# Second memory attention of an encoder kernel, in pairs of heads woven into the projection slots

## What is computed

```python
def memory_attention(q, mem_k, mem_v):
    s = jnp.einsum('bthd,bmhd->bhtm', q, mem_k).astype(jnp.float32) * (MEM_HEAD_DIM ** -0.5)
    p = jax.nn.softmax(s, axis=-1).astype(mem_v.dtype)
    o = jnp.einsum('bhtm,bmhd->bthd', p, mem_v)
    return o.reshape(q.shape[0], q.shape[1], MEM_WIDTH)
...
            u = rms_norm(h, odd_norm1[j])
            q, k, v, g, zf, zb, qm = jnp.split(u @ odd_w_in[j], splits, axis=-1)
...
            mo = memory_attention(qm.reshape(B, T, MEM_HEADS, MEM_HEAD_DIM), mem_k, mem_v)
            h = h + jnp.concatenate([mix, mo], axis=-1) @ odd_w_out[j]
            h = h + moe_swiglu(rms_norm(h, odd_norm2[j]), odd_w_router[j], odd_w_gate[j], odd_w_up[j], odd_w_down[j])
```

## Time and profile before

| | |
|---|---|
| three runs | 1540.44, 1543.67, 1546.06 us; median 1543.67 |
| the profiled execution | 1542.09 us, its span 1540.3 us |
| TensorE | 1482.5 us busy, 96% of the span |
| VectorE, ScalarE | 1176.5 us (76%), 977.2 us (63%) |
| DMA queue of the weights | 427.79 MB, 77.4% of 16 engines |
| from G2's end to the first GLA product | 426.31 to 465.25 us |

### The profile page before, as it was taken

The page is one execution under the profiler, slowest core; times in us unless marked ns, Lnnn a source line. Parts: engine busy times, 40 slices in busy tenths (PEclk is TensorE's granted clock), DMA queues, the critical chain, the costliest instruction groups (busy, mean ns, idle before and its releaser), DMA issues.

```text
span 1540.3 us, 20865 instructions
## 1 busy us (share of the span) xinstructions
PE 1482.5 (96%) x7832; PEld 1256.6 (82%) x7832; DVE 1176.5 (76%) x1004; ACT 977.2 (63%) x907; POOL 20.5 (1%) x41
## 2 busy tenths in 40 slices
PE   5999999999988899999999999999999999999997
PEld 5985899998976688888888888888888888888885
DVE  4457554445556588888888889888889898888887
ACT  3337434443652377777777777777777777777775
POOL 1000000000001000000000000000000000000000
PEclk9999999999999899999999999999999999999999
DMA  7650465644350589989989989989998998998982
GB/s 271 228 165 1 142 203 191 191 149 128 125 191 28 192 323 381 375 313 379 370 312 377 368 316 371 379 313 369 377 366 319 378 371 311 377 372 310 382 318 94
DMA packets 198731, 428.41 MB, mean 278 GB/s; under 512 B 9534, under 2 KB 39580, under 8 KB 198685
## 3 DMA queue, kind: packets, MB, share of 16 engines
q1 hardware_dynamic: 198684, 427.79, 77.4%
HBM read 426.71 MB, written 1.05 MB: 278 GB/s over the span
## 4 chain that ended last, share of the span: by engine, by line
PE 89%; DVE 4%; ACT 3%; issue 2%; SPq 0%; DMA 0%; POOL 0%; DVEq 0%; ACTq 0%; POOLq 0%
PE ps L1234 27%; PE ps L1236 27%; PE ps L1235 27%; PE ps L1616 1%; DVE w_lo L1182 1%; PE ps L1335 1%; PE ps L1585 1%; ACT w_hi L717 1%; PE ps L1660 1%; PE ps L1309 1%; PE ps L1346 1%; PE ps L1255 1%; PE ps L1323 1%; ACT w_hi L514 0%; PE ps L1553 0%
## 5 line engine op out<-in xcount | busy, mean ns | idle before, releaser
L1182 DVE TENSOR_TENSOR w_lo<-raw,w_hi 128x2048 fp32r<-128x2048 f32 (+1 forms) x224 | 442.6, 1985 | 61.5 <-ACT w_hi L717 61.0
L717 ACT ACTIVATE w_hi<-raw 128x2048 fp32r<-128x2048 f32 (+1 forms) x224 | 372.7, 1672 | 130.3 <-PE ps L1236 130.2
L1234 PE MATMUL ps<-w_hi,xt_hi 128*128 128x512 f32 (+2 forms) x1080 | 418.5, 387 | 3.7 <-DVE xt_lo L1069 1.5
L1236 PE MATMUL ps<-w_hi,xt_lo 128*128 128x512 f32 (+2 forms) x1080 | 411.8, 381 | 0.0
L1235 PE MATMUL ps<-w_lo,xt_hi 128*128 128x512 f32 (+2 forms) x1080 | 410.9, 380 | 0.0
L1182 DVE TENSOR_TENSOR w_lo<-arena,w_hi 128x2048 fp32r<-128x2048 f32 x144 | 295.7, 2053 | 29.5 <-ACT w_hi L717 29.0
L717 ACT ACTIVATE w_hi<-arena 128x2048 fp32r<-128x2048 f32 x144 | 248.6, 1726 | 82.4 <-PE ps L1236 82.2
L821 DVE TENSOR_TENSOR w_lo<-raw,w_hi 128x2048 fp32r<-128x2048 f32 (+2 forms) x69 | 149.7, 2172 | 165.3 <-ACT w_hi L514 165.2
L1234 PEld LDWEIGHTS ps<-w_hi,xt_hi 128*128 128x128 f32 x1080 | 203.6, 189 | 44.5 <-issue 3.8
L1236 PEld LDWEIGHTS ps<-w_hi,xt_lo 128*128 128x128 f32 x1080 | 203.4, 188 | 38.4
L1235 PEld LDWEIGHTS ps<-w_lo,xt_hi 128*128 128x128 f32 x1080 | 203.9, 189 | 35.2
(11 more groups left out here) (204 smaller groups left out, 1205.4 us busy)
## 6 DMA issues: line engine op xcount, KB each, us to landing
raw<-exp_gate SPq DMA_DIRECT2D x74, 1024.0 KB, 5.8
raw<-exp_up SPq DMA_DIRECT2D x48, 1024.0 KB, 5.7
arena<-exp_down SPq DMA_DIRECT2D x48, 1024.0 KB, 5.6
arena<-exp_up SPq DMA_DIRECT2D x40, 1024.0 KB, 7.2
raw<-exp_down SPq DMA_DIRECT2D x40, 1024.0 KB, 6.3
arena<-exp_gate SPq DMA_DIRECT2D x24, 1024.0 KB, 6.8
raw<-exp_up SPq DMA_DIRECT2D x32, 512.0 KB, 4.8
raw<-even_gate SPq DMA_DIRECT2D x11, 1024.0 KB, 5.3
```

The source lines that it names most:

```text
L717: ins = act.activation(w_hi[:, n % CUT, at:at + src.shape[1]], src, ACT.Copy)
L1182: ins = dve.tensor_tensor(w_lo[:, n % CUT, cols], src, w_hi[:, n % CUT, cols].bitcast(F32), ALU.subtract)
L1234: pe.matmul(dst, a[0], b[0], start=start, stop=False, skip_group_check=shared)
L1236: return pe.matmul(dst, a[1], b[0], start=False, stop=stop, skip_group_check=shared)
```

## The change

- The factor 1/8 moves into ScalarE's copy of the memory queries (`qm1`), so the scores need no scaling. VectorE takes the maximum and ScalarE the exponential straight from the bank of the scores; the two scaled copies of each head are gone.
- The heads go in pairs. Both heads' scores are multiplied together, the two row halves of the array in turn; the two heads' products with the values likewise, the two column halves in turn.
- The pairs start one block sooner: scores of the first pair between G2 and G3, its transposes and the scores of the second pair between V0 and V1, its product behind V1, the transposes of the second pair between V2 and V3, its product behind V3.
- Turned probabilities have two banks, 6 and 7. The second half of V2 and V3 goes to bank 0 in place of bank 7, so V2 now waits for the copies of V0 and V1 (`in1_copied_a` 6, `in1_copied_v` 3).
- V0 waits for the first Silu eviction (`in1_copied_a` 4), no longer for the second. ScalarE takes the exponentials of the first pair ahead of the second Silu, and those of the second pair behind it.
- The second pair's scores wait for the exponentials of the first, which read the same banks.

```diff
--- before.py
+++ after.py
@@ -619,7 +619,8 @@
                 return ps[0:DK, bank, :].rearrange("p (h t) -> p h t", h=2)
 
             products(I_Z + 1)
-            act.activation(qm1.rearrange("p i t -> p (i t)"), ps[:, 5, :], ACT.Copy).then_inc(in1_copied_a, 1)
+            act.activation(qm1.rearrange("p i t -> p (i t)"), ps[:, 5, :], ACT.Copy,
+                           scale=float(HEAD) ** -0.5).then_inc(in1_copied_a, 1)
             products(I_Q + 1)
             act.activation(qg[0:DK, 0:2, :], pair_of(qg, 0), ACT.Copy, scale=float(DK) ** -0.5).then_inc(in1_copied_a, 1)
             for i in range(4):
@@ -654,19 +655,46 @@
             for d in range(2):
                 act.wait_ge(kd_turned, 2 * d + 2)
                 act.activation(kdt[:, d], ps[:, 4 + 2 * d:6 + 2 * d, 0:KW], ACT.Copy).then_inc(kdt_ready, 1)
+            def mem1_exp(p):
+
+                for i in (16 + 2 * p, 17 + 2 * p):
+                    act.wait_ge(scores_max, i + 1)
+                    if i == 19:
+                        act.wait_ge(probs_turned, 17)
+                    for t in range(TT):
+                        act.activation(s_b[:, i % 3, t, :], ps[:, 4 + i % 2, T * t:T * (t + 1)], ACT.Exp,
+                                       bias=stat[:, i, t, 0:1],
+                                       accum_out=stat[:, i, t, 1:2]).then_inc(probs_exp, 1)
+
+            def mem1_probs(p):
+
+                for i in (16 + 2 * p, 17 + 2 * p):
+                    act.wait_ge(probs_turned, i + 1)
+                    if p == 1:
+                        act.wait_ge(heads_done, i - 1)
+                    act.activation(pT_b[:, i % 2].rearrange("p j q -> p (j q)"), ps[:, 6 + i % 2, :],
+                                   ACT.Copy).then_inc(probsT_ready, 1)
+
+            def mem1_high(p):
+
+                act.wait_ge(heads_done, 18 + 2 * p)
+                act.activation(hT_hi[:, 0, T * p:T * (p + 1)], ps[:, 3, 0:T], ACT.Copy).then_inc(mix_hi, 1)
+
+            high_to(I_V + 1)
+            mem1_exp(0)
             gates_silu(1)
-            attention(16, 4, s_b, pT_b, range(0, 1))
-            high_to(I_V + CUT)
-            attention(16, 4, s_b, pT_b, range(1, 2))
+            high_to(I_V + 3)
+            mem1_probs(0)
+            mem1_exp(1)
             act.wait_ge(slot_done, I_V + 2)
             act.activation(v1[:, 0, 0:384], ps[:, 0, 0:384], ACT.Copy).then_inc(in1_copied_a, 1)
-            high_to(I_V + 1 + CUT)
-            attention(16, 4, s_b, pT_b, range(2, 3))
-            high_to(I_V + 2 + CUT)
-            attention(16, 4, s_b, pT_b, range(3, 4))
+            high_to(I_V + 4)
+            mem1_high(0)
+            high_to(I_V + 5)
+            mem1_probs(1)
             act.wait_ge(slot_done, I_V + 4)
             act.activation(v1[:, 0, 384:768], ps[:, 2, 0:384], ACT.Copy).then_inc(in1_copied_a, 1)
-            attention(16, 4, s_b, pT_b, range(4, 7))
+            mem1_high(1)
             high_to(I_V + 3 + CUT)
 
             def heads_high(b):
@@ -996,24 +1024,50 @@
                     dve.wait_ge(exps_done, 2 * d + x + 1)
                     dve.tensor_tensor(dst[0:DK, d], dst[0:DK, d], src[0:DK].rearrange("p h t -> p (h t)"),
                                       ALU.mult).then_inc(qk_ready, 1)
-            low_to(I_G + 3 + CUT)
-            attention(16, 4, s_b, 8, range(0, 1))
-            low_to(I_V + CUT)
+            def mem1_max(p):
+
+                for i in (16 + 2 * p, 17 + 2 * p):
+                    dve.wait_ge(scores_done, i + 1)
+                    dve.tensor_reduce(stat[:, i, :, 0], ps[:, 4 + i % 2, :].rearrange("p (t m) -> p t m", t=TT), AX_X,
+                                      ALU.max, negate=True).then_inc(scores_max, 1)
+
+            def mem1_norm(p):
+
+                for i in (16 + 2 * p, 17 + 2 * p):
+                    dve.wait_ge(probs_exp, 2 * i + 2)
+                    mark(dve.reciprocal(stat[:, i, :, 2], stat[:, i, :, 1]))
+                    settle()
+                    for t in range(TT):
+                        dve.tensor_scalar(s_b[:, i % 3, t, :], s_b[:, i % 3, t, :], stat[:, i, t, 2:3], None,
+                                          ALU.mult).then_inc(probs_ready, 1)
+
+            def mem1_low(p):
+
+                dve.wait_ge(mix_hi, 9 + p)
+                dve.tensor_tensor(hT_lo[:, 0, T * p:T * (p + 1)], ps[:, 3, 0:T],
+                                  hT_hi[:, 0, T * p:T * (p + 1)].bitcast(F32), ALU.subtract).then_inc(mix_lo, 1)
+
+            low_to(I_V)
+            mem1_max(0)
+            low_to(I_V + 1)
+            mem1_norm(0)
+            low_to(I_V + 2)
             dve.wait_ge(gnorm_in, 16)
             sg8 = sg.rearrange("p t (h n) -> p (t h) n", n=DV)
             dve.wait_ge(in1_copied_a, 5)
             dve.tensor_tensor(sg8, sg8, gnb[:].unsqueeze(1).broadcast_to([P, TT * GH, DV]),
                               ALU.mult).then_inc(sgn_ready, 1)
-            attention(16, 4, s_b, 8, range(1, 2))
+            mem1_max(1)
+            low_to(I_V + 3)
+            mem1_norm(1)
             dve.wait_ge(slot_done, I_V + 2)
             dve.tensor_copy(v1[:, 1, 0:384], ps[:, 1, 0:384]).then_inc(in1_copied_v, 1)
-            low_to(I_V + 1 + CUT)
-            attention(16, 4, s_b, 8, range(2, 3))
-            low_to(I_V + 2 + CUT)
-            attention(16, 4, s_b, 8, range(3, 4))
+            low_to(I_V + 4)
+            mem1_low(0)
+            low_to(I_V + 5)
             dve.wait_ge(slot_done, I_V + 4)
-            dve.tensor_copy(v1[:, 1, 384:768], ps[:, 7, 0:384]).then_inc(in1_copied_v, 1)
-            attention(16, 4, s_b, 8, range(4, 8))
+            dve.tensor_copy(v1[:, 1, 384:768], ps[:, 0, 0:384]).then_inc(in1_copied_v, 1)
+            mem1_low(1)
 
             def o_norm(i):
 
@@ -1479,18 +1533,61 @@
                 ins.then_inc(kd_turned, 1)
             pe.wait_ge(in1_copied_a, 3)
             pe.wait_ge(in1_copied_v, 2)
-            by_token(I_G + 2, (2, 3))
-
-            attention1 = (16, 4, pT_b, lambda i: qm1[:, (i - 16) // 2, :], lambda i: mkT[:, (i - 16) // 2, :],
-                          lambda i, j: mv[:, j, HEAD * (i - 16):HEAD * (i - 15)], 8)
+            def mem1_scores(p):
+
+                if p == 1:
+                    pe.wait_ge(probs_exp, 2 * 17 + 2)
+                for t in range(TT):
+                    for a in range(2):
+                        r = slice(HEAD * a, HEAD * (a + 1))
+                        ins = pe.matmul(ps[:, 4 + a, T * t:T * (t + 1)], qm1[r, p, tok[t]], mkT[r, p, :],
+                                        start=True, stop=True)
+                        if t == 1:
+                            ins.then_inc(scores_done, 1)
+
+            def mem1_turn(p):
+
+                for i in (16 + 2 * p, 17 + 2 * p):
+                    pe.wait_ge(probs_ready, 2 * i + 2)
+                    if p == 1:
+                        pe.wait_ge(probsT_ready, i - 1)
+                    for t in range(TT):
+                        for j in range(2):
+                            o = T * j + P * t
+                            ins = pe.transpose(ps[:, 6 + i % 2, o:o + P], s_b[:, i % 3, t, P * j:P * (j + 1)], ident)
+                    ins.then_inc(probs_turned, 1)
+
+            def mem1_out(p):
+
+                pe.wait_ge(probsT_ready, 18 + 2 * p)
+                if p == 1:
+                    pe.wait_ge(mix_lo, 9)
+                for j in range(2):
+                    for a in range(2):
+                        r = slice(HEAD * a, HEAD * (a + 1))
+                        hd = 2 * p + a
+                        ins = pe.matmul(ps[r, 3, 0:T], mv[:, j, HEAD * hd:HEAD * (hd + 1)], pT_b[:, a, j, :],
+                                        start=(j == 0), stop=(j == 1), skip_group_check=True)
+                        if j == 1:
+                            ins.then_inc(heads_done, 1)
+
+            by_token(I_G + 2, (2, 3), halves=range(1))
             pe.wait_ge(kdt_ready, 2)
-            attention(*attention1, range(0, 1))
+            mem1_scores(0)
+            by_token(I_G + 2, (2, 3), halves=range(1, 2))
+            pe.wait_ge(in1_copied_a, 4)
+            by_token(I_V, (0, 1), halves=range(1))
+            mem1_turn(0)
+            mem1_scores(1)
+            by_token(I_V, (0, 1), halves=range(1, 2))
             pe.wait_ge(in1_copied_a, 5)
-            for c, banks in enumerate(((0, 1), (2, 7))):
-                for half in range(2):
-                    by_token(I_V + 2 * c, banks, halves=range(half, half + 1))
-                    attention(*attention1, range(2 * c + half + 1, 2 * c + half + 2))
-            attention(*attention1, range(5, 7))
+            mem1_out(0)
+            pe.wait_ge(in1_copied_a, 6)
+            pe.wait_ge(in1_copied_v, 3)
+            by_token(I_V + 2, (2, 0), halves=range(1))
+            mem1_turn(1)
+            by_token(I_V + 2, (2, 0), halves=range(1, 2))
+            mem1_out(1)
 
             def state_products(i):
                 for d in range(2):
```

## The result

| | before | changed |
|---|---|---|
| median of the runs | 1544.74 us (4 runs, 1540.44 to 1546.06) | 1532.72 us (4 runs, 1531.72 to 1533.16) |
| ratio to before | | 0.9926, 95% interval 0.9912 to 0.9940 |
| span of the profiled execution | 1540.3 us | 1529.9 us |
| first product of G2 to first state product ("the stage") | 422.06 to 465.25: 43.19 us | 423.47 to 455.77: 32.30 us |
| from there to the end | 1075.05 us | 1074.13 us |

The changed kernel is faster, by 11.4 us going by the ratio. The page of the profile still has TensorE holding 89% of the chain, as in the earlier trace rows; its busy time fell from 1482.5 to 1475.2 us.

A forecast was written before the change was run, and what follows sets the result against it. The prediction took TensorE, holding 89% of the chain of waits, as the bound; its terms on TensorE's list summed to 9.9 us, so 1543.67 - 9.9 = 1533.8 us for the median, range 1529 to 1540.

The forecast's parts named there:

- four waits go: TensorE's waits for second Silu, head 16's normalization, turned-probability copy and bank 3's cut all vanish: 4.54 us.
- slow stretch goes: TensorE stays at 2.4 GHz where 5.98 us ran at half clock: 2.99 us won, bounds 0 and 2.99.
- scores in pairs: Two heads' scores on alternating row halves cost about 1.2 us a pair, against 4.45 for four heads: 2.05 us won.
- products with the values: Two heads on the two column halves cost 1.25 us; both pairs together win 0.75 us, bounds 0 and 1.0.
- slots: TensorE's dense blocks, as many of each kind as before, cost the same within 0.1 us: nothing won.
- wait for both key copies: First scores, now right after G2, wait for ScalarE's copies freeing banks 4 to 7: 0.74 us lost.
- Rival C: The pairs of scores do not overlap on TensorE: 2 x 1.06 us more, 1535.9 us; chance 0.08.
- The chain to V2: ScalarE's and VectorE's work up to V1's bank copy ends at 444.05, wanted at 444.45: 0.4 us slack, tightest place.
- B: ScalarE's and VectorE's chain becomes the bound at V2, as table load and exponentials take longer: 1535 to 1537; chance 0.18.
- sum for a drain: If each ScalarE table switch also drains some 1380 ns, V2 is about 1.0 us later and the gain 8.9 us.
- rival F: Slower: the new wait at 427 and half-array products keep the whole stage at 1.2 GHz, 1562 us; chance 0.04.
- E: The gain is lost to a later, unseen wait behind the stage: 1540 to 1545 us; chance 0.05.

The follow-up runs named there:

- a_late: Changed kernel with two more 128x512 copies on ScalarE ahead of the second pair's exponentials; stage 33.22 us, median 1534.94 us, ratio 0.9948 to before.
- b_same: Kernel before, unchanged, profiled a second time; stage 43.39 us, 1543.56 us in one run.
- b_direct: Kernel before with the factor 1/8 in the query copy and maximum and exponential read from the scores' bank; stage 40.63 us, ratio 0.9983.
- b_banks: Kernel before with two banks of turned probabilities, V2 and V3 in banks 2 and 0; stage 42.50 us, ratio 0.9979.
- b_both: Kernel before with softmax straight from the bank and two banks of turned probabilities, heads still one by one; stage 39.99 us, ratio 0.9971.
- b_fill: Kernel before with 18 identity transposes into unused bank 3 where TensorE waits 2.11 us ahead of head 17's transposes; stage 43.15 us, ratio 0.9987.
- a_silu: Changed kernel, but V0 waits again for the second Silu eviction; stage 38.80 us, median 1537.49 us, ratio 0.9960 to before.
- b_v0: Kernel before, but V0 waits for the first Silu eviction only and V2 for the second; stage 40.49 us, median 1543.84 us, ratio 0.9998.

## Why the prediction was right

The forecast was 1533.8 us, in 1529 to 1540; it is 1532.72. That the two lie 1.1 us apart is in part luck: the gain was put at 9.9 us and is 11.4 by the ratio, and the median of before has moved up by 1.07 with a fourth run. The stage, where the working can be followed, was to win 9.9 us and won 10.89. Term by term:

| term | predicted | measured | from |
|---|---|---|---|
| four waits go | 4.54 | 4.54 | none of them left; the sum is of the rows before |
| slow stretch goes | 2.99 | 2.99 | clock 1.00 over the stage |
| scores in pairs | 2.05 | 2.31 | 4.45 less twice 1.07 |
| products with the values | 0.75 | 1.21 | 1.00 + 1.00 + 1.25 (the first put at full clock) less twice 1.02 |
| transposes | 0.34 | 0.36 | 0.41 + 0.51 + 0.53 + 0.66 less 0.96 and 0.79 |
| slots | 0 | 0.20 | G3 to V3: 21.60 us before (V3 put at 4.25 for full clock, an estimate: the rest of the 2.99), 21.40 after |
| wait for both key copies | -0.74 | -0.72 | ahead of the first scores |
| sum | 9.93 | 10.89 | |

- *Overlap was under-sized.* The step that missed is "products with the values": I took 1.25 us for a pair from the one row in which two heads stood together (464.00 to 465.25). That row was misread. The second of the two heads waited in it for ScalarE's copy of its turned probabilities, which ended at 464.20; its first record starts at 464.25, 0.25 us behind the other head's, and those 0.25 are what the pair cost over a head alone:

```profile
463.60 0.60 ACT L550 ACTIVATE states<-ps 128x512 f32<-128x512 f32 x1 [0.20 <-PE ps L1323]
```

With both copies there, a pair costs 1.02, a head alone 1.00. The pairs of scores were put too high as well: 0.53 us for 1000 columns, the price read from the GLA's row, gives 1.09 us for their 2048 columns, not 1.2, and they took 1.07. The lower bounds, 1.06 and 1.0, were about the values for both. Of this the Trainium skill, TensorEngine Tiling (Array Packing), Key Properties, says that different tiles execute their weight loads and products in parallel; 1.07 us for two heads against 1.06 for one agrees. Rival C, no overlap, did not come.
- *The chain to V2* was right to 0.2 us: counted from G2's first product, the copy's end was forecast at 21.99 us and came at 21.76. V2's start was forecast at 22.39 and came at 21.88, 0.5 sooner, since two pairs of scores and the product ahead of it were faster (0.26 and 0.23). So the slack was 0.1 in place of 0.4. a_late shows that B's mechanism is real; it had not come into effect, but only just. In the sum for a drain, 8.9 us, one load was left out: 1.4 us more ahead of Silu too would have ended Silu at 437.5 where V0 ends at 436.8, 0.7 us later, so V2 would have been 1.7 us late and the sum 8.2.
- *The clock.* The sum of this term held, but not all of what I said of it. Against rival F I argued that the wait of 1.27 us had not brought the clock down before. In other executions of the same stage it did: in five of the six profiles with that wait the clock fell in V0 (b_same, and b_direct, b_banks, b_both and b_fill, whose V0 took 5.9 us or a little more). The two profiles of before lost some 3 us each to the clock, in different places. What is shown: in six profiles of changed kernels whose longest wait in the stage is under 1 us, the clock never fell in it, and with a wait of 3.75 us put back it fell right behind (a_silu). What stays open is whether each single wait brings it down: in b_v0 one of 2.10 us did not, and b_fill was spoilt as a test of it. The terms of the waits and of the clock are not independent either: they add up to the stage because its rows do, but a kernel before that kept its clock would have waited some 1.1 us more at head 18, as b_fill and b_v0 do.
- *Behind the stage* the gain came through, but only to within the clock of the GLA: over all fourteen profiles the rest of the program took 1072.8 to 1074.5 us where that was 1.00, 1074.9 to 1076.7 where it was 0.86 or 0.93, and 1078.0 to 1080.0 where it was 0.80 or 0.81. Neither E nor F came.

Each part of the change brings little alone, because the waits hid each other. Each of b_direct, b_banks and b_v0 took a wait away and found another at head 18: 0.24 us for ScalarE's copy of head 17, 0.80 for VectorE's normalization, and 1.09 for the copy again. All four are gone only in the changed kernel, where the steps are fewer and stand further apart.

## What to carry to other kernels

Small attention work between dense blocks cost this kernel more by waits and half clock (4.54 and 2.99 us) than by what pairing saved on its products (2.31 and 1.21): put a whole block between each two steps of a pair, and pair what uses half of the array's rows or columns, since here two halves cost what one did (1.07 and 1.02 us against 1.06 and 1.00). Price each handover of the new order by rows and look for the smallest slack: here it was 0.1 us, and 1 us more on ScalarE came straight through. Before a row's length is taken as a price, see whether an input of its later instructions came in the middle of it: the 1.25 us of a pair held 0.25 of waiting that no bracket showed. And when the engine that a bracket names had long been done, look for the other semaphore. A gain of 1 us in a stage cannot be judged by the program's time when the clock behind it moves that by up to 7 us; compare the stage's own rows, and profile the same kernel twice.

## What was not expected of the hardware

- Four fp32 products on two row halves took 1.07 us both when the halves alternated in the list and when each half's two stood together; in the second case a product began ahead of one that stands before it in the list.
- Two profiles of one unchanged kernel had the clock fall in different places: at 452.62 only, or at some 433 and at 454. In b_v0 it stayed at half for most of 18.2 us (0.53) while TensorE was busy for 16.66 of them.
- Reading the scores from the bank instead of SBUF cost neither engine more: an exponential of 128x256 took 0.48 us (0.51 before), and two maxima 1.29 us (0.69 each before).
